# Fourteen of the sixteen merge gate tiles of w_in by seven block products

## The reference, cut to what matters

```
h = rmsnorm(x, g_mix[l]) * (1.0 + sc_a) + sh_a              # 1024 tokens x 1024
z = h @ w_in[l] + b_in[l]
(cb, cc, cu, q, kc, vc, k_s, v_s, k_w, v_w, nsa_g, merge_g) = jnp.split(z, split_at, axis=-1)
y_conv = short_conv_mixer(cb, cc, cu, conv_w[l]) @ w_up_conv[l]
y_attn = nsa_mixer(...) @ w_up_attn[l]
g_conv, g_attn = jnp.split(jax.nn.sigmoid(merge_g), 2, axis=-1)   # 1024 columns each
mixed = (g_conv * y_conv + g_attn * y_attn) @ w_o[l]
x = x + ga_a * mixed
h = rmsnorm(x, g_mlp[l]) * (1.0 + sc_m) + sh_m
x = x + ga_m * (jnp.square(jax.nn.relu(h @ w_ff1[l])) @ w_ff2[l])
```

## Time and profile before

| | |
|---|---|
| time, median of 3 runs | 3293.94 us (3293.86 to 3295.71) |
| time of the profiled execution | 3295.99 us |
| its span, first to last instruction | 3294.2 us |
| granted TensorE clock, mean | 0.986 of full speed |
| PE busy | 3177.3 us, 96% |
| PEld, DVE, POOL, ACT busy | 79%, 56%, 47%, 30% |
| DMA | 264.16 MB, mean 80 GB/s |

### The profile page before, as it was taken

How to read it: one execution, slowest core, us unless ns; L and a number is a source line. 1 busy time by engine, 2 the same in 40 slices (tenths; PEclk the granted TensorE clock), 3 DMA queues, 4 the chain that set the end, 5 groups by cost and what they waited for, 6 DMA issues and landing times.

```text
span 3294.2 us, 40452 instructions
## 1 busy us (share of the span) xinstructions
PE 3177.3 (96%) x15213; PEld 2594.2 (79%) x15213; DVE 1853.5 (56%) x2507; ACT 972.2 (30%) x1771; POOL 1541.3 (47%) x1727
## 2 busy tenths in 40 slices
PE   8999999998899999999999999999979999999998
PEld 6888887676787888888778888867758888888887
DVE  7533246887546665555565332478864545555555
ACT  2100114666222222222220001256661222222223
POOL 3433332323453556666744333323334556666665
PEclk7999999999899999999999999999999999999999
DMA  7333621000522222111243345200005121111112
GB/s 262 118 114 129 188 75 39 1 1 1 198 63 73 83 76 66 52 52 52 74 146 97 121 141 173 58 20 1 1 15 203 48 61 52 52 52 52 52 52 96
DMA packets 294440, 264.16 MB, mean 80 GB/s; under 512 B 10347, under 2 KB 274791, under 8 KB 293736
## 3 DMA queue, kind: packets, MB, share of 16 engines
q1 hardware_dynamic: 279410, 207.66, 21.2%
q10 hardware_dynamic: 14838, 53.94, 4.3%
HBM read 223.81 MB, written 30.41 MB: 77 GB/s over the span
## 4 chain that ended last, share of the span: by engine, by line
PE 88%; DVE 7%; issue 2%; ACT 2%; POOL 0%; ACTq 0%; DVEq 0%; POOLq 0%
PE lin L1186 57%; PE lin L1535 16%; PE aux L1426 2%; DVE pTL L2117 2%; PE pv L1442 2%; PE pv L1443 1%; DVE negm L2093 1%; PE lin L1402 1%; PE lin L1403 1%; PE pv L1291 1%; ACT pTH L1753 1%; PE lin L1368 1%; PE lin L1236 0%; PE lin L1237 0%; PE lin L1238 0%
## 5 line engine op out<-in xcount | busy, mean ns | idle before, releaser
L1157 POOL TENSOR_SCALAR unit<-wraw 128x512 fp32r<-128x512 f32 x396 | 322.5, 814 | 1015.0 <-PE lin L1186 694.6
L1186 PE MATMUL lin<-hH,unit 128*128 128x512 f32 x2272 | 718.1, 393 | 11.5 <-POOL wlo L1159 6.1
L1186 PE MATMUL lin<-hL,unit 128*128 128x512 f32 x2272 | 712.8, 390 | 0.0
L1186 PE MATMUL lin<-hH,wlo 128*128 128x512 f32 x2272 | 712.3, 390 | 0.0
L1159 POOL TENSOR_TENSOR wlo<-wraw,unit 128x512 fp32r<-128x512 f32 x396 | 564.5, 1425 | 33.0
L1186 PEld LDWEIGHTS lin<-hH,unit 128*128 128x128 f32 x2272 | 424.8, 189 | 100.2 <-issue 8.0
L1186 PEld LDWEIGHTS lin<-hH,wlo 128*128 128x128 f32 x2272 | 427.8, 188 | 90.2
L1186 PEld LDWEIGHTS lin<-hL,unit 128*128 128x128 f32 x2272 | 428.1, 188 | 89.8 <-issue 0.2
L1535 PE MATMUL lin<-fH,unit 128*128 128x512 f32 x1568 | 486.0, 390 | 0.6 <-DVE xT L2253 0.6
L2253 DVE SCALAR_TENSOR_TENSOR xT<-lin,adac,xT 128x512 f32<-128x512 f32 x448 | 328.6, 748 | 180.5 <-PE lin L1535 176.0
L1103 POOL TENSOR_SCALAR prob<-prob,fac 128x640 f32<-128x640 f32 (+7 forms) x256 | 182.5, 713 | 441.3 <-DVE fac L2087 423.4
(11 more groups left out here) (282 smaller groups left out, 4479.3 us busy)
## 6 DMA issues: line engine op xcount, KB each, us to landing
wraw<-in_w_ff SPq DMA_DIRECT2D x136, 512.0 KB, 4.0
wraw<-in_w_ada SPq DMA_DIRECT2D x80, 512.0 KB, 3.7
wraw<-in_w_in SPq DMA_DIRECT2D x78, 512.0 KB, 5.0
wraw<-in_w_o SPq DMA_DIRECT2D x24, 512.0 KB, 3.9
adar<-in_w_ada SPq DMA_DIRECT2D x16, 512.0 KB, 11.6
x_keep<-xT ACTq DMA_DIRECT2D x4, 2048.0 KB, 8.6
mix_keep<-tmp ACTq DMA_DIRECT2D x16, 512.0 KB, 3.1
gate_keep<-ropes ACTq DMA_DIRECT2D x16, 512.0 KB, 6.7
```

The lines of the kernel that those rows point to most:

```text
L1157: pool.tensor_scalar(high, raw, 1.0, 1.0, ALU.mult, ALU.mult).then_inc(w_hi, 1)
L1186: mm = pe.matmul(lin[c % 2][:, hf], w, m(k, hf), start=first, stop=last)
```

## The change

Of the 16 gate tiles, `ga0` and `ga1` stay dense. The other 14 become seven pairs ("mate" and "wide", `GATES`, `WIDE`). A pair is a matrix of 1024 x 256, cut in four blocks of 512 x 128; with the four blocks of `h` (features in halves, tokens in halves) it is computed by seven products of 12 matmuls in place of 96 matmuls (`wide_products`). POOL makes four sums of weight blocks into `wsum` and seven low parts (`wide_forms`), ACT seven high parts (`wide_high`). The sums of activation blocks are made once a layer: DVE makes four sums `t1` to `t4` in eight pieces (`hf_piece`) and their low parts (`hf_low`), ACT their high parts (`hf_high`). ACT copies four of the partial products out of PSUM (`copy_product`), DVE adds the others to them (`gate_sums`), and ACT takes the sigmoid.

The order becomes: conv tiles, `ga0`, the four `uc` tiles, `ga1`, seven pairs, `kc`. The `uc` products are stored without their gate; they are fetched again when their gates are ready (`fetch_y`, `gate_products`). The 32 `w_ada` tiles of that part now all lie before the pairs: two behind each of the last six conv tiles and three behind each `uc` tile. The pairs' raw tiles use places 2, 3, 4 and a sixth, `xraw` (slot `RAW`), in the memory of conv's operands. The loads of the compression's weights move behind `q1` and `q2`, and the small tables' loads behind the pairs.

In the MLP the ring of eight units begins with `w_ff1`'s third tile (`ADA_FROM = 2`); the first two use five raw places. The 16 `w_ada` tiles there begin two tiles later. `last_high` and `last_low` are issued two by two, one and two quads earlier.

```
+ADA_FROM = 2
+ADA_CONV = ((0, 2, 1), (1, 1, 1), (2, 2, 2), (2, 2, 2))
+ADA_GATE, ADA_UP = 1, 3
+GATES = [("ga", i) for i in range(2, KC)] + [("gc", i) for i in range(KC)]
+WIDE = len(GATES) // 2
+RAW_WIDE = (2, 3, 4, RAW)
...
-                dense("w_in", 0, off + P * j, [(name, j)], {("cc", 0): 0, ("cu", 0): 2}.get((name, j), 1))
+                dense("w_in", 0, off + P * j, [(name, j)], ADA_CONV[j][m])
+        dense("w_in", 0, O_MG + D, [("ga", 0)], ADA_GATE)
         for i in range(0, KC, 2):
-            dense("w_in", 0, O_MG + P * i, [("gc", i)], 1)
-            dense("w_in", 0, O_MG + P * (i + 1), [("gc", i + 1)], 1)
-            dense("w_up_conv", 0, P * i, [("uc", i), ("uc", i + 1)], 1)
-        for i in range(KC):
-            dense("w_in", 0, O_MG + D + P * i, [("ga", i)], 1)
+            dense("w_up_conv", 0, P * i, [("uc", i), ("uc", i + 1)], ADA_UP)
+        dense("w_in", 0, O_MG + D + P, [("ga", 1)], ADA_GATE)
+        for q in range(WIDE):
+            for kind, (g, i) in zip(("mate", "wide"), GATES[2 * q:2 * q + 2]):
+                tiles.append((kind, layer, "w_in", 0, O_MG + D * (g == "ga") + P * i, KC, ("gates", q)))
...
-        if name == ("f1", 0):
-            ff = True
+        if name == ("f1", ADA_FROM):
+            mode, unit = "pairs", UNITS_W - 2
+        if t[0] == "mate" and mode != "wide":
+            mode, at, unit = "wide", 0, max(HI_AT[SPLIT[-1]]) + 1
...
+        if mode == "wide":
+            s = RAW_WIDE[at % len(RAW_WIDE)]
+        else:
+            while mode == "pairs" and at % RAW not in RAW_FF or name == ("ua", 0) and at % RAW != RAW - 2 or name == ("ga", 1) and at % RAW != RAW - 1:
+                at += 1
+            s = at % RAW
...
+                def wide_forms(q):
...
+                    if q == 0:
+                        pool.wait_ge(lin_done, CHUNK[layer, ("uc", KC - 1)] + 1)
+                        for i in range(4):
+                            form_sum(0, i)
+                    form_low(0, a11)
+                    form_low(1, s1)
+                    form_low(2, a12)
+                    form_low(3, s2)
+                    if q + 1 < WIDE:
+                        form_sum(q + 1, 0)
+                    form_low(4, s4)
...
+                def wide_products(q):
...
+                    for i in range(PRODUCTS):
+                        if q == 0 and i in HF_READY:
+                            pe.wait_ge(hf_lo, 8 * layer + HF_READY[i])
+                        pe.wait_ge(form_lo, PRODUCTS * p + i + 1)
+                        if q == 0 and i in (0, 2):
+                            c = CHUNK[layer, ("ga", 1)] - (i == 2)
+                            pe.wait_ge(lin_free[c % 2], c // 2 + 1)
+                        if q and i == 0:
+                            pe.wait_ge(g_add, w0 - 3)
...
+                        for k in range(4):
+                            for w, m in ((wh, mh), (wh, ml), (wl, mh)):
+                                mm = pe.matmul(bank, w[:, k * P:(k + 1) * P], m[:, k, :], ...)
+                        mm.then_inc(prod_done, 1)
...
+                    if i % 2:
+                        hf_high(2 + i // 2)
+                wide_high(0, 0)
+                wide_high(0, 1)
+                hf_high(6)
+                wide_high(0, 2)
+                hf_high(7)
+                gate(1)
+                wide_high(0, 3)
...
+                ada_tiles_of(ADA_UP)
+                hf_piece(5)
+                hf_low(4)
+                ada_tiles_of(ADA_GATE)
+                hf_low(5)
+                done(dve, ("uc", KC - 1))
+                hf_piece(6)
+                hf_low(2)
+                hf_piece(7)
+                hf_low(3)
+                hf_low(6)
+                hf_low(7)
...
-                        if fg == NFG - 2:
-                            last_low(q)
+                        if fg == NFG - 2 and q in (1, 2):
+                            last_low(2 * q - 2)
+                            last_low(2 * q - 1)
```

More of the change, by code:

```diff
@@ L162, in ff1 @@
                 dense("w_ff1", 0, P * f, [("f1", f)])
-                for g, t in [x for x in [next(ahead, None)] if x]:
+                for g, t in [x for x in [next(ahead, None) if f >= ADA_FROM else None] if x]:
                     tiles.append(("ada", layer + 1, g, t))
@@ L1064, in sync @@
                         sp.wait_ge(v_done, N_VGROUPS)
+                    if SLOT[n] == RAW:
+                        sp.wait_ge(lin_done, CHUNK[layer, ("uc", KC - 1)] + 1)
                     load_tile(sp, n)
@@ L1113, in form_sum @@
                     def form_sum(i, x, y, op):
-                        if FORM_PRIOR[n][i]:
-                            released(pool, FORM_PRIOR[n][i])
+                        for before in FORM_PRIOR[n][i]:
+                            released(pool, before)
                         pool.tensor_tensor(form_part(unitF, n, i, 1), x, y, op).then_inc(w_sum, 1)
@@ L1331, in tensor @@
                 mm.then_inc(par_t, 1)
-                dense("kc", H, L)
-                ada(None)
                 dense("vc", H, L)
@@ L1577, in scalar, with hf_high @@
                 act.wait_ge(x_out[1], 16)
+                gate_first = CHUNK[layer, ("ga", 1)] % 2
+                gate_home = [lin[(gate_first + i // 2) % 2][:, half[i % 2]] for i in range(4)]
+                cbuf = fbuf[:, :, :].rearrange("p a (b t) -> p (a b) t", b=2)
+                def hf_high(m):
+                    act.wait_ge(hf_sum, 8 * layer + m + 1)
+                    ks = slice(2 * (m % 2), 2 * (m % 2) + 2)
+                    high, full = ((t1H, t1F), (t2H, t2F), (t3H, t3F), (t4H, t4F))[m // 2]
+                    act.activation(high[:, ks, :], full[:, ks, :], ACT.Copy).then_inc(hf_hi, 1)
                 def fetch_tables():
@@ new lines, in gate_store @@
+                def gate_store(q):
+                    for j in range(2):
+                        kind, i = GATES[2 * q + j]
+                        if kind == "ga":
+                            act.wait_ge(g_sig, 4 * (wide0 + q) + 2 + 2 * j)
+                            act.dma_start(gate_keep[i], ropes[:, j, :]).then_inc(gate_out[j], 16)
+                        else:
+                            act.wait_ge(g_mix, KC * layer + i + 1)
+                            act.dma_start(mix_keep[i], tmp[:, j, :]).then_inc(mix_out[j], 16)
@@ new lines, in fetch_y @@
+                def fetch_y(q):
+                    for j in range(2):
+                        kind, i = GATES[2 * q + j]
+                        if kind == "gc":
+                            act.wait_ge(mix_out[j], 16 * KC * layer + 16 * (KC // 2 + i // 2))
+                            act.dma_start(tmp[:, j, :], mix_keep[i]).then_inc(y_in, 16)
+                act.wait_ge(cv_lo, v0 + CONV_W // P)
+                gate(0)
+                hf_high(1)
+                for i in range(KC):
+                    if i >= 2:
+                        act.wait_ge(mix_out[i % 2], 16 * KC * layer + 16 * (i // 2))
+                    done(act, ("uc", i))
+                    act.activation(tmp[:, i % 2, :], slot(("uc", i))[:, :], ACT.Copy).then_inc(free_sem(("uc", i)), 1)
+                    freed(act, ("uc", i))
+                    act.dma_start(mix_keep[i], tmp[:, i % 2, :]).then_inc(mix_out[i % 2], 16)
+                    if i % 2:
+                        hf_high(2 + i // 2)
@@ new lines, in hf_low, with ada_tiles_of @@
+                def hf_low(m):
+                    dve.wait_ge(hf_hi, first_h + m + 1)
+                    dve.wait_ge(hf_sum, first_h + m + (3, 5, 1, 1)[m // 2])
+                    ks = slice(2 * (m % 2), 2 * (m % 2) + 2)
+                    high, low, full = ((t1H, t1L, t1F), (t2H, t2L, t2F), (t3H, t3L, t3F), (t4H, t4L, t4F))[m // 2]
+                    dve.tensor_tensor(low[:, ks, :], full[:, ks, :], high[:, ks, :].bitcast(F32), ALU.subtract).then_inc(hf_lo, 1)
+                def ada_tiles_of(count):
+                    for _ in range(count):
+                        ada()
```

392 lines of the change are left out of this document (283 added, 109 removed).

## The result

The changed kernel takes 3301.72 us (median of 12 runs, 3297.63 to 3306.83) against 3293.86 (12 runs, 3291.36 to 3299.48): ratio 1.0023 with a 95% interval of 1.0014 to 1.0032. It is slower by some 8 us, where 22 us less were forecast. Its profiled execution took 3299.39 us, at the low end of its runs, so the two traces show only 3.5 us of it (spans 3297.7 and 3294.2). One stretch in which these kernels hardly differ, from the first product of layer 1's attention to the MLP's first seven products, takes 536.6 to 544.9 us in the fourteen traces of this case; so the times of kernels are compared by their medians, and traces only stretch by stretch.

What follows compares the result with a forecast made beforehand. TensorE, busy for 96% of the span, was taken as the bound. Gains of 52.7 us less losses of 30.8 made 21.9 us less, forecast 3272 us (chance 0.60); range 3251 to 3290, with 0.2 outside.

Steps and rivals of the forecast that it cites:

- Fewer matmuls: Gate tile pairs: 84 matmuls in place of 96 gain 2.88 us in each of 14 pairs, 40.3 us.
- list of what it costs at nothing: Pairs' work on POOL, ACT and DVE, plus fetches and stores: all hidden under other work, 0 us.
- `ga1` late: Before ga1: PE idles for its late load, 6.5 us in layer 0 and 7.0 in layer 1.
- The first product: Start of the pairs: waits for ACT's reading of ga1 behind DVE's last pieces, 5.9 us lost per layer.
- rival of strict turns: Start of the pairs: DVE and POOL never overlap, 2.40 us per addition, 3.2 us more per layer, 3278 us; chance 0.12.
- The `uc` stretch: Three w_ada tiles behind each uc tile: 3 us lost over both layers (0 to 8).
- The MLP's start: Layer 0, first w_ff1 tiles: two waits and half clock go, 7.4 us gained (4 to 11.4).
- The MLP's end: Earlier last_low takes DVE's hL off PE's path: 5.0 us gained (3.5 to 5.3).
- `kc` in layer 1: At kc in layer 1, POOL's operations stand in PE's way: 2.2 us lost.
- the small ones: Losses of 2.2 us at kc in layer 1 and 0.3 at a load of the MLP's last tiles: 2.5 us.

Runs made afterwards that it cites:

- rotate_first: Changed kernel with the value compression's eight loads moved behind q3's load and kc's rotation on SP's queue: 3290.52 us, ratio 0.9989 to the kernel before.
- ga1_early: Changed kernel with ga1's load right behind the last uc tile's, ahead of the last four w_ada tiles: 3302.57 us, ratio 1.0025 to the kernel before.
- pool_waits: Changed kernel with POOL starting the first pair's sums only after DVE finished all eight activation pieces: 3305.26 us in one run.
- gate_early: Changed kernel with ACT reading ga1 ahead of the second half of t4's high part: 3288.98 us, ratio 0.9985 to the kernel before.
- five_places_undone: Changed kernel with w_ff1's first tiles in three raw places again and w_ada tiles from the first on: 3309.57 us, ratio 1.0047 to the kernel before.
- gate_first: Changed kernel with kc's rotation and ga1's load earlier, w_ada tiles moved into conv, ACT reading ga1 and POOL's first low part earlier: 3267.09 us, ratio 0.9916.
- last_low_as_before: Changed kernel with last_high and last_low one a quad again, as in the kernel before: 3302.32 us, ratio 1.0021 to the kernel before.

## Why the prediction was wrong

Two steps failed. The sum had nothing for what stood behind the moved compression loads in SP's queue (11.7 us), and it under-priced the start of the pairs (13.9 us): `ga1`'s arrival, the first product's wait, and the half clock behind that wait, for which there was no term.

**Fewer matmuls: right.** The pairs run at 2.72 us per product with no wait for POOL in them, as said. They took 135.4 us a layer in place of 133.3, the 2 us being half clock at their start: so 36.1 us came and not 40.3, and the 4.2 us are a cost that the sum left out. It counted the half clock behind `ga1`, and none behind the first product's wait.

**The compression: the step that failed by its absence.** The description of the change names the move of these loads behind `q1` and `q2`; the prediction priced no queue entry behind them. Queued behind them on SP is the rotation of `kc`, on which DVE's rope, the blocks and PE's compression hang. The stretch grew by 8.6 and 3.1 us in the traces: 7.30 and 2.06 of it are this wait, 1.21 and 1.00 the wait at L1479 for a table whose load the change also moved. The prediction's list of what it costs at nothing, with its cover, names neither. rotate_first takes the first of them away, and the median falls by 11 us.

**`ga1` late: right in kind, under-sized.** 8.26 and 9.83 us against 6.5 and 7.0. The layer 0 value is the 8.4 of the earlier trace rows, which I had put down as the worst case; I built 6.5 from a transfer's median and POOL's time alone, though POOL's operation at 251.72 took 2.12 us there, not 1.29. ga1_early shows that the whole of it hid a second bound: taking the wait away gained nothing.

**The first product: right in kind, under-sized.** It stood 20.6 and 19.4 us behind `ga1`'s start, against my 17.2. The six additions came 2.24 us apart, not 1.87: from 259.06 to 272.48 in layer 0 and from 1880.90 to 1894.34 in layer 1. In layer 0 DVE was also free for them only at T + 5.1, not T + 3.6. In the earlier trace rows every second operation of POOL was the short `unit` one, 0.62 us when alone; in the forms all of them have two operands and take 1.27. So my pitch was a mean over a mixture that doesn't stand here. The rival of strict turns came nearer: it lost 9.1 us per layer, and 9.3 and 8.1 were lost. In part that is luck, since its 2.40 us for a pair of operations is above the 2.24 measured, while its 1.14 for an addition alone is under the 1.25 that pool_waits shows. By that rule of the Trainium skill ("SBUF — State Buffer", section "SBUF: two separate sides"), a VectorE instruction with two SBUF inputs and a GpSimd one that reads SBUF hold one port pair one at a time, each for its whole instruction. pool_waits agrees in kind: an addition takes 1.25 us alone and 2.2 beside POOL, 0.3 less than the 2.52 that it and POOL's 1.27 add up to. The price of it in the end was ACT's order: gate_early took the wait away without touching DVE.

**The `uc` stretch: about right in layer 0** (0.54 and 0.60 us of waits), and some 2 us in layer 1, a remainder: what is left of its stretch when the other terms are taken off.

**The MLP's start: under-sized on the other side.** 11.7 us came, my bound of 11.4 and not 7.4. I had taken layer 1's stretch (48.98 us) as what is left; layer 0 of the change does it in 44.60 (973.99 to 1018.59 in the chain). Layer 1's has another cause of its own, which I didn't look for. five_places_undone splits it: 8.7 for the places, and 3.0 that came with the rest of the change.

**The MLP's end: half of it wrong.** 2.0 us in all, not 5. The low parts were put inside the last pair, where the additions to `xT` follow PE at every product; a 2.2 us operation there comes straight back as waits. What was won in layer 1 is mostly clock.

**`kc` in layer 1: right**, 2.31 us against 2.2.

Forecast and trace lie 25.4 us apart (21.9 less, 3.5 more). The compression makes 11.7 of it and the two starts of the pairs 13.9 (`ga1` 4.6, the first product 5.6, the half clock behind it 4.2, the `uc` stretch half a microsecond less than priced). The MLP's end makes 2.7 (0.3 of loss had been priced there), and its start takes 4.3 back; the remaining 1.4 lies in stretches that nothing was forecast for. That gate_first ends at 3267 us, near the forecast's 3272, confirms nothing: it also moves `w_ada` tiles and POOL's first low part, which the prediction did not have. The outer bounds of the losses in the sum, 15.1 and 47.5, are a few tenths off: with the small ones at 2.5 the terms' own bounds add up to 15.4 and 47.1.

## What to carry to other kernels

When a block of loads is moved in a queue, list what stood behind its new place and price that, small copies first: 512 KB of rotated rows behind 4 MB of weights cost PE 7.3 us in one layer and 2.1 in the other. When an engine's in-order queue holds one instruction that frees a bank beside others that wait for a slow producer, put the freeing one first. And a contended duration is to be read off a stretch where the other engine does the same kind of operation, without gaps.

## What the runs showed of the hardware

Additions of 128 x 1024 with two SBUF inputs on DVE and operations of 128 x 512 with two inputs on POOL slow each other: each starts every 2.2 us when both have work, 1.25 and 1.27 us when alone (pool_waits; POOL from 276.57 to 279.04). The trace shows this as longer instructions on both engines, not as idle time between them.

While the 16 DMA engines are busy, issuing takes the queue long: two issues of 256 KB took SP 1.30 us at 388.39 in the kernel before; eight took 12.18 us at 412.39 in the changed kernel and 5.29 us at 439.58 in rotate_first, with the DMA engines busy all through both.

PE's granted clock over the 5 to 6 us behind idle time (0.50 is 1.2 GHz all through, 1.00 is 2.4 GHz): 0.50 behind 6.1 us (the kernel before) and 9.8 us, 0.61 behind 6.6 and 0.64 behind 8.3; 0.65 and 0.66 behind 4.6 us, 0.58 behind 3.65 (rotate_first, 1892.33). Behind 2.3 to 2.6 us it went either way: 0.50 in gate_first (261.09), 0.68 in layer 1 of the kernel before and 0.69 and 0.68 in last_low_as_before, but 1.00 in layer 0 of the kernel before (1622.81) and at `kc` in the changed kernel (2034.04). Behind 1.73 us (gate_early) it stayed 1.00.
